# A hybrid decoder step on one core: five edits to the order of its instructions

## The reference

```python
h = rms_norm(x, norm1_g)                      # D_MODEL = 1024
q, k, v, u, vs, ga, gb = split(h @ w_in)      # 512,128,128,512,512,1024,1024
u  = gelu(u)
vs = layer_norm(gelu(vs), ln_v_g, ln_v_b)     # 4 groups of 128 channels
oa = window_attention(q, k, v, sinks)         # window 128, 8 heads, 2 kv heads
ob = u * (causal(w_spatial) @ vs + b_spatial) # within chunks of 128 positions
h  = sigmoid(ga) * (oa @ w_branch_a) + sigmoid(gb) * (ob @ w_branch_b)
x  = x + h @ w_out
# then the mixture of experts: norm, a group of 4, two of its 4 experts,
# silu(h @ gate) * (h @ up) * weight, @ down, added into x
```

## Time and profile before

| | |
|---|---|
| median of three runs | 914.64 us (911.8 to 917.33) |
| the profiled execution | 916.96 us |
| its span | 915.0 us |
| mean granted clock of PE | 0.988 of full speed |
| busy: PE, DVE, ACT, POOL | 96%, 62%, 43%, 28% |
| DMA | 153.55 MB, mean 168 GB/s |

### The profile page before, as it was taken

The page is one execution under the profiler, slowest core; times in us unless marked ns, Lnnn a source line. Parts: engine busy times, 40 slices in busy tenths (PEclk is TensorE's granted clock), DMA queues, the critical chain, the costliest instruction groups (busy, mean ns, idle before and its releaser), DMA issues. The chain is left out here.

```text
span 915.0 us, 16885 instructions
## 1 busy us (share of the span) xinstructions
PE 878.8 (96%) x5635; PEld 785.5 (86%) x5636; DVE 563.1 (62%) x1033; ACT 392.5 (43%) x724; POOL 253.0 (28%) x250
## 2 busy tenths in 40 slices
PE   7999999999999999999999999999789999999994
PEld 7777775888998999999999999999778888887883
DVE  5687876543488755655433955445877757577561
ACT  5666655211254444333211212223527657576551
POOL 2434332334231000000001540000152456355562
PEclk9999999989999999999999999999999999999998
DMA  8433431340522422223883237863558989989733
GB/s 278 139 102 107 126 82 30 98 188 24 189 67 85 165 99 103 94 95 99 295 311 96 72 103 264 304 221 95 164 153 305 334 273 295 325 245 343 243 55 47
DMA packets 79552, 153.55 MB, mean 168 GB/s; under 512 B 10701, under 2 KB 44173, under 8 KB 78960
## 3 DMA queue, kind: packets, MB, share of 16 engines
q1 hardware_dynamic: 72000, 134.84, 42.6%
q0 software_dynamic: 7488, 17.85, 8.6%
HBM read 122.80 MB, written 40.30 MB: 178 GB/s over the span
## 5 line engine op out<-in xcount | busy, mean ns | idle before, releaser
L1475 POOL TENSOR_TENSOR hT_lo_raw<-hT_lo_raw,arena 128x1056 f32<-128x1056 f32 x7 | 23.3, 3326 | 226.4 <-DVE arena L1721 226.4
L2466 DVE TENSOR_TENSOR hT_lo<-room,hT_hi (+1 forms) x32 | 72.1, 2291 | 17.3 <-ACT hT_hi L2155 17.3
L79 PE MATMUL psum<-w_hi,hT_hi 128*128 128x512 f32 (+3 forms) x216 | 79.7, 369 | 1.7 <-DVE hT_lo L1096 1.0
L79 PE MATMUL psum<-hT_hi,x_xT_hi 128*128 (+1 forms) x192 | 77.9, 406 | 1.9 <-DVE x_xT_lo L2618 1.2
L80 PE MATMUL psum<-w_lo,hT_hi 128*128 128x512 f32 (+3 forms) x216 | 75.9, 351 | 0.0
L81 PE MATMUL psum<-w_hi,hT_lo 128*128 128x512 f32 (+3 forms) x216 | 75.8, 351 | 0.0
L80 PE MATMUL psum<-hT_lo,x_xT_hi 128*128 (+1 forms) x192 | 75.8, 395 | 0.0
L81 PE MATMUL psum<-hT_hi,x_xT_lo 128*128 (+1 forms) x192 | 75.8, 395 | 0.0
L2095 POOL DMA_INDIRECT out_y<-y,put_at x23 | 50.0, 2172 | 90.7 <-DMA out_y<-y,put_at 74.8
L2155 ACT ACTIVATE hT_hi<-room (+1 forms) x32 | 59.9, 1923 | 12.0 <-PE psum L81 10.1
L1515 ACT ACTIVATE arena<-arena 128x264 f32<-128x264 f32 x64 | 26.9, 425 | 80.9 <-DVE arena L1710 80.3
(11 more groups left out here) (413 smaller groups left out, 2629.7 us busy)
## 6 DMA issues: line engine op xcount, KB each, us to landing
room<-in_w_gu SPq DMA_DIRECT2D x16, 2048.0 KB
dn_raw<-in_w_dn SPq DMA_DIRECT2D x16, 1024.0 KB, 8.5
arena<-in_w_ab SPq DMA_DIRECT2D x24, 512.0 KB, 4.3
gate_rows<-arena SPq DMA_DIRECT2D x32, 264.0 KB, 2.2
arena<-gate_rows SPq DMA_DIRECT2D x16, 528.0 KB, 4.5
xT_chunk<-in_xT SPq DMA_DIRECT2D x8, 528.0 KB, 3.9
x_in<-in_x SPq DMA_DIRECT2D x8, 512.0 KB, 5.3
h_rows<-h_raw SPq DMA_DIRECT2D x8, 512.0 KB, 4.0
```

The source lines that it names most:

```text
L79: eng.matmul(out, lh, rh, start=first and k == 0, stop=False)
L1475: pool.tensor_tensor(here, here, part[v % 2], ALU.add).then_inc(h2_summed, 1)
L2466: dve.tensor_tensor(gu_lo[:, buf, ks], gu_raw[:, buf, ks], gu_hi[:, buf, ks].bitcast(F32), ALU.subtract).then_inc(gu_lo_made.sem, 1)
```

## The change

Five edits, none of which alters what is computed:

1. PE's order in the attention tail: the halves of v(3) and v(4) stand between mix(0) with the first kv head of the sample's values, the second head with mix(1), and the turn of the sample's output; mix(3) follows mix(2) at once. ACT does gelu(2) and gelu(3) before it splits the first u weights; DVE normalises v(2) before it divides the sample's output.
2. DVE's order in the dense head: the first and second sums one u step later, S3 behind low(1), both fourth sums behind low(3).
3. SP's queue in the last gate turn: one row of gates is loaded before the second store, one behind it, two behind all four.
4. `FIRST_K` 3 in place of 2.
5. POOL's last scatter-add counts on a semaphore of its own, for which SP waits; the waits for the gathers come before it, and POOL waits at the end for the other adds alone.

```diff
--- before.py
+++ after.py
@@ -37,7 +37,7 @@
 TC = NTOK // 3
 HALF = NTOK // 2
 HC = HALF // 2
-FIRST_K = 2
+FIRST_K = 3
 ARENA = SG * NTOK + 4 * KD * P + 2 * (KD // 2) * HALF + 4 * TC + 2 * (KD // 2) * P
 NG, EPG = 4, 4
 NE = NG * EPG
@@ -656,12 +656,13 @@
             ins.then_inc(sp_made, 1)
             gelu(0)
             gelu(1)
+            gelu(2)
+            gelu(3)
             act.wait_ge(so_made, 1)
             act.wait_ge(first_in, DMA)
             act.activation(first_u[1][:, :, :], first_u[0][:, :, :], ACT.Copy).then_inc(first_hi_made, 1)
-            gelu(2)
             oa_high(PT)
-            for i in range(3, NT):
+            for i in range(4, NT):
                 gelu(i)
 
         @block.tensor
@@ -826,16 +827,16 @@
                     mm = pe.transpose(bank(psum, 2 + kv)[0:NS, P:2 * P], s_scores[kv][:, WIN:], ident[:, :])
                 mm.then_inc(spT_made, 1)
 
-            def sample_values():
+            def sample_values(kv):
                 pe.wait_ge(spT_copied, 1)
                 pe.wait_ge(v_cache_in, DMA)
                 pe.wait_ge(o_scaled, PT)
-                for kv in range(KV):
-                    d = slice(kv * HD, (kv + 1) * HD)
-                    for b in range(DEC_B):
-                        pe.matmul(bank(psum, 5)[:, d], pT_s[kv][:, b * P:(b + 1) * P], v_cache[:, b, d], start=b == 0, stop=False)
-                    mm = pe.matmul(bank(psum, 5)[:, d], pT_n[kv][0:NS, :], v_ring[0:NS, PT % 4, d], start=False, stop=True)
-                mm.then_inc(so_made, 1)
+                d = slice(kv * HD, (kv + 1) * HD)
+                for b in range(DEC_B):
+                    pe.matmul(bank(psum, 5)[:, d], pT_s[kv][:, b * P:(b + 1) * P], v_cache[:, b, d], start=b == 0, stop=False)
+                mm = pe.matmul(bank(psum, 5)[:, d], pT_n[kv][0:NS, :], v_ring[0:NS, PT % 4, d], start=False, stop=True)
+                if kv == KV - 1:
+                    mm.then_inc(so_made, 1)
 
             def sample_o_turn():
                 pe.wait_ge(so_copied, 1)
@@ -940,14 +941,18 @@
             sample_turn()
             for half in range(2):
                 v_product(2, half)
+            v_product(3, 0)
             mix(0)
-            sample_values()
-            for half in range(2):
-                v_product(3, half)
+            sample_values(0)
+            v_product(3, 1)
+            sample_values(1)
             mix(1)
+            v_product(4, 0)
             sample_o_turn()
+            v_product(4, 1)
             mix(2)
-            for i in range(4, NT):
+            mix(3)
+            for i in range(5, NT):
                 for half in range(2):
                     v_product(i, half)
                 mix(i - 1)
@@ -1207,6 +1212,7 @@
             step.did(dve.reciprocal(rden[:, 0, 0:KV], rden[:, 0, 0:KV]))
             v_normalise(1)
             add_bias(0)
+            v_normalise(2)
             dve.wait_ge(so_made, 1)
             for kv in range(KV):
 
@@ -1215,7 +1221,6 @@
                     ins = dve.tensor_scalar(o_sb[0:NS, g, kv, :], bank(psum, 5)[q, kv * HD:(kv + 1) * HD], rden[q, 0, kv:kv + 1], None,
                                             ALU.mult)
             ins.then_inc(so_copied, 1)
-            v_normalise(2)
             add_bias(1)
             dve.wait_ge(first_hi_made, 1)
             dve.tensor_tensor(first_u[2][:, :, :], first_u[0][:, :, :], first_u[1][:, :, :].bitcast(F32),
@@ -1443,11 +1448,14 @@
                 load_weights(n + 2)
                 store(n, 2, 0, 0, e1, c11_out)
                 if n == TURNS - 1:
-                    for v in range(4):
-                        load_sig(v)
+                    load_sig(0)
                 store(n, 4, 1, 1, out, c22_out)
+                if n == TURNS - 1:
+                    load_sig(1)
                 store(n, 6, 1, 0, u3, c21_out)
                 store(n, 8, 0, 1, out, c12_out)
+            for v in range(2, 4):
+                load_sig(v)
             load_weights(TURNS + 2)
             sp.wait_ge(m_made, passed(GATES - 1))
             for o, name in zip(oaT, ("oa_hi", "oa_lo")):
@@ -1729,10 +1737,10 @@
                 if u in (0, 3, 6):
                     u_low(u // 3 + 1)
                 u_step(u)
-                if u in (1, 2):
-                    first_sums(u - 1)
-                if u in (3, 4):
-                    second_sum(u - 3)
+                if u in (2, 3):
+                    first_sums(u - 2)
+                if u in (4, 5):
+                    second_sum(u - 4)
                 if u in (5, 6, 7):
                     n = (1, 3, 2)[u - 5]
                     for piece in range(2):
@@ -1740,14 +1748,15 @@
                 if u == US - 4:
                     low(0)
                 if u == US - 3:
-                    for name in ("S1", "S2", "S3"):
+                    for name in ("S1", "S2"):
                         weight_sum(0, name)
                 if u == US - 2:
                     low(1)
-                    fourth_sum(0)
+            weight_sum(0, "S3")
             low(2)
             low(3)
-            fourth_sum(1)
+            for piece in range(2):
+                fourth_sum(piece)
             weight_sum(0, "S4")
             dve.wait_ge(ob_lo, US)
             for g in range(GATES):
@@ -1892,6 +1901,7 @@
         turned, routed = sem("turned"), sem("routed")
         lgT_copied, lg_turned, constants_made, front_made = sem("lgT_copied"), sem("lg_turned"), sem("constants_made"), sem("front_made")
         turned_first, last_kept, last_half_made = sem("turned_first"), sem("last_kept"), sem("last_half_made")
+        last_added = sem("last_added")
         y_copied, y_rest, squared, summed = sem("y_copied"), sem("y_rest"), sem("squared"), sem("summed")
         pool_step, zeros_made, w_r_zeroed = sem("pool_step"), sem("zeros_made"), sem("w_r_zeroed")
         sample_squared, gained = sem("sample_squared"), sem("gained")
@@ -2041,6 +2051,7 @@
                 down_landed(i)
                 if i + 1 < NE:
                     load_down(i + 1)
+            sp.wait_ge(last_added, DMA)
 
         @block.gpsimd
         def _(pool):
@@ -2102,16 +2113,16 @@
 
             def last(used):
                 pool.tensor_copy(last_at[:, 0:1], scatter_at[:, bass.ds(used - 1, 1)]).then_inc(at_copied.sem, 1)
+                others = pool.value_load(step_plan[0:1, 1, PLANNED:PLANNED + 1], min_val=NE - 1, max_val=MOST_STEPS - 1)
                 at_copied.wait(pool, used - 1)
+                for r in range(RING):
+                    pool.wait_ge(gathered[r], (used + (2 * RING - 1 - r)) // RING * DMA)
                 out_made.wait(pool, used - 1)
                 pool.wait_ge(last_half_made, 1)
                 pool.sem_inc(passed, 1)
                 pool.indirect_dma_start(io["y"], bass.IndirectOffsetOnAxis(last_at[:, 0:1], 0), last_out, None,
-                                        bounds_check=NTOK - 1, oob_is_err=False, compute_op=ALU.add).then_inc(added, DMA)
-                pool.wait_ge(added, used * DMA)
-
-                for r in range(RING):
-                    pool.wait_ge(gathered[r], (used + (2 * RING - 1 - r)) // RING * DMA)
+                                        bounds_check=NTOK - 1, oob_is_err=False, compute_op=ALU.add).then_inc(last_added, DMA)
+                pool.wait_ge(added, others * DMA)
 
...
```

## The result

The changed kernel takes 908.02 us (median of 20 runs, 906.6 to 914.73) against 914.69 for the kernel before (20 runs): a ratio of 0.9934, 95% interval 0.9915 to 0.9952. The medians differ by 6.7 us; the ratio makes it 6.0, between 4.4 and 7.8. The forecast was 910.4 us, a gain of 6.6 taken off the profiled execution of before (916.96), and not off the median. Against that base the gain is larger: the profiled execution of the changed kernel took 907.48 us, 9.5 less.

The account below looks back on a forecast made before the run. PE was taken as the bound, busy nearly all the span, with the chain of waits mostly through its products. Terms 2.0 + 0.5 + 1.1 + 0.4 + 2.6 = 6.6 off 916.96 gave 910.4 us, range 906.4 to 914.5.

Parts of the forecast that it names:

- The base: Whole kernel: gains come off the profiled execution's 916.96 us, its 2.3 us surplus over the median left in.
- Attention tail, 2.0: PE order in the attention tail: v(5) 3.7 us earlier, less 1.7 for a short clock fall; range -1.5 to 3.7.
- Rival a: Attention tail: the clock never falls, as wide halves between thin groups keep it up; 908.7 us, chance 0.24.
- Rival c: Attention tail: clock falls in mix(0) and values(0), half products don't raise it; 920.3 us, chance 0.06.
- Dense head, 0.5: DVE order in the dense head: PE waits shrink until low(4) is late next; gain 0.5 us, -1.0 to 2.8.
- Rival d: Dense head: sums compete with weights, low(4) or a product near it waits 1.5 us more; 911.9 us, chance 0.11.
- Gate loads, 1.1: SP's queue in the last gate turn: PE's 1.09 us gate wait goes; gain 1.1 us, bounds 0 to 1.1.
- FIRST_K, 0.4: Barrier into the last phase: nine products move ahead, covering part of PE's 1.06 us idle; gain 0.4, -0.2 to 1.06.
- The end, 2.6: Kernel end: POOL's DRAIN starts at 907.9 instead of 910.5, its 4.318 us its own; gain 2.6, bounds 0 and 2.6.
- Rival b: Kernel end: DRAIN ends a fixed time after the last landing or descriptor; 913.0 us, chance 0.24.

Follow-up runs that it names:

- experiment 2: The changed kernel with the attention edit undone and the other four edits kept: 909.94 us, ratio 0.9954.
- experiment 6: The changed kernel with FIRST_K 2 in place of 3: 908.61 us, ratio 0.9951.
- experiment 5: The changed kernel with the four gate loads back ahead of the second store: 909.35 us, ratio 0.9951.
- experiment 4: The changed kernel with the old order of sums in the dense head: 908.67 us, ratio 0.9946.
- experiment 10: The changed kernel with POOL's wait for the other adds moved to ACT, with one small activation behind it: 907.89 us, ratio 0.9936.
- experiment 8: The changed kernel with low(4) on DVE moved ahead of the weight sum S4 and t_low(4,0): 907.56 us, ratio 0.9932.
- experiment 9: The changed kernel with the old end, the last scatter-add counted with the others and POOL waiting for it: 910.21 us, ratio 0.9968.

## Why the prediction was right, point by point

The time that was forecast, 910.4, is 2.4 us above the measured median, and the 6.6 us of the sum agree with the 6.7 between the medians by luck: on the sum's own base, the profiled executions, 9.5 came.

By medians the five terms, each undone in turn, are 1.9, 0.65, 1.3, 0.6 and 2.2 us, together 6.7, against 2.0, 0.5, 1.1, 0.4 and 2.6. By the ratios they are 1.8, 1.1, 1.6, 1.6 and 3.1, together 9.1. Each is the difference of two figures with intervals of nearly 2 us to either side, so the agreement is better than the measurement can vouch for; the traces say what is right in it.

- **The base.** The sum starts from 916.96 and keeps its surplus of 2.3 us over the median. The fall in the tail does not explain that surplus: by their mean clock most runs of before have the fall, and so has the median. The 5 runs at 0.988, the clock of the profiled one, have a median of 916.26, the 7 at 0.990 have 914.52 (of the 20 beside experiment 2): the lower clock goes with the longer time, but where it was lower no trace shows.
- **Attention tail, 2.0.** The wait before mix(3) was forecast as 1.9 (by its own numbers 197.4 - 195.6 = 1.8) and is 1.71; v(5) as 198.4 and is 198.84. The step that failed is the clock's fall behind this wait, priced at 1.7: nine profiles have the wait, none a fall behind it. Where a fall comes, in three of eleven profiles, it comes earlier, behind mix(0) and values(0), and lasts the 3.4 us that were priced, which is luck. And the term has no one size: against an execution of before with the fall the edit gains 3.3, against one without it loses 1.2. On the kernel before, alone, it gave nothing that can be measured; in the presence of the others 1.9. Both are mixtures over executions, and their intervals overlap.
- **Rival a** (no fall in the tail, 908.7) is what the profiled execution after shows, but its reason, that wide halves between the thin groups keep the clock up, does not hold in the three profiles with a fall.
- **Rival c** needed a fall in mix(0) and values(0) that half products don't end. In experiment 6 the fall came just behind them, and it was over before the first half product ended.
- **Dense head, 0.5.** Right in kind: low(4) is late next, with a wait of 1.28. The trace gives 1.2 since DVE's own waits shrank too: the one of 3.38 for a DMA is 1.53. Rival d's loss did not come.
- **Gate loads, 1.1.** Right: 1.1 by the trace of experiment 5, 1.4 between the profiles of before and after; no gap opened behind it.
- **FIRST_K, 0.4.** Right: 0.76 at the barrier, 0.3 to 0.7 with the wait for the weights behind it; the edge at the weights is where it was put.
- **The end, 2.6.** Right: 2.4, with DRAIN at 4.316 us. Rival b is wrong for this change, but only just: by experiments 4, 6 and 10 its bound stands close behind. The Trainium skill, "VectorE: DVE Perf Modes" (The DRAIN you can't avoid), gives about 12 ns for the DRAINs of the runtime's preamble and postamble; POOL's at the end of this block, 4.3 to 7.1 us in these profiles, is not of that kind.

## What to carry to other kernels

When a profiled execution holds a stretch at low clock, ask whether all runs have it, before a term is built on removing it: the runs' own mean clocks give a first sign. A wait removed inside one full queue can come back as a wait for the last thing in that queue, so that only the slack there is gained. Work that needs nothing late, such as the waits and the DRAIN of the last engine, is best started before the last transfer, down to the next bound.

## What the runs showed of the hardware

With one order of PE's products in the attention tail, the granted clock fell there in one execution and not in another: 0.57 from 178 to 190 us in the profile of before, 1.00 in that of experiment 2. The cost was 4.5 us by v(5) (202.13 against 197.63), and 2.8 us between the medians of the two groups of runs (13 and 7 of 20, by their mean clock). The stretch in the routing stage comes and goes as well: 3.4 us at half in the profiles of before and after, none from 630 to 660 us in those of experiments 8, 9 and 10. The changed kernel's own spread, 906.6 to 914.73 at mean clocks of 0.993 to 0.996, follows the clock little: the runs of 907.08 and 914.73 both had 0.993.

POOL's DRAIN at the end took 4.316 to 4.318 us in nine of the eleven profiles in which it began more than 2 us behind the issue of the last add, 4.336 and 4.469 in the other two, and 6.783 to 7.087 us in the three in which it began ahead of that add's record.
